# Weight splits put ahead of the tile that each step takes, in a 2-layer hybrid decoder step

## What is computed

```python
h = rmsnorm(x, w['norm1_g'])
(q_m, k_m, v_m, i_pre, f_pre, o_pre, glu_a, glu_b, q_a, k_a, v_a, g_pre) = split_cols(h @ w['w_in'])
y_a = (sigmoid(o_pre) * mlstm(q_m, k_m, v_m, i_pre, f_pre)) @ w['w_mlstm_out']
y_b = silu(layernorm(dwconv(glu_a * sigmoid(glu_b)))) @ w['w_conv_out']
y_c = sliding_window_attention(rope(q_a), rope(k_a), v_a) @ w['w_attn_out']
x = x + (g_a * y_a + g_b * y_b + g_c * y_c) @ w['w_out']
h2 = rmsnorm(x, w['norm2_g'])
gp, up = h2 @ w['w_ffn_gate'], h2 @ w['w_ffn_up']
x = x + (silu(dwconv3(gp)) * up) @ w['w_ffn_down']
```

## Time and profile before

| | us |
|---|---|
| median of 3 runs | 1123.89 (1120.84 to 1132.49) |
| the profiled execution | 1123.45 |
| its span | 1121.7 |
| mean granted TensorE clock in it | 0.968 |
| TensorE busy, 7950 matmuls | 1058.4 (94%) |
| VectorE busy | 795.8 (71%) |
| ScalarE busy | 538.8 (48%) |

### The profile page before, as it was taken

How to read it: one execution, slowest core, us unless ns; L and a number is a source line. 1 busy time by engine, 2 the same in 40 slices (tenths; PEclk the granted TensorE clock), 3 DMA queues, 4 the chain that set the end, 5 groups by cost and what they waited for, 6 DMA issues and landing times.

```text
span 1121.7 us, 19458 instructions
## 1 busy us (share of the span) xinstructions
PE 1058.4 (94%) x7950; PEld 1004.1 (90%) x7950; DVE 795.8 (71%) x1433; ACT 538.8 (48%) x951; POOL 68.0 (6%) x65
## 2 busy tenths in 40 slices
PE   5999999999898999999979999999997989999997
PEld 3988889888798999999979897898887989999996
DVE  4576986855698677775555879777648867887663
ACT  3545553424634555553344555542274536666432
POOL 0020000213100000000000200002230000000000
PEclk9999999989899999999989999999989989999998
DMA  9654545254455575555566564363454547665561
GB/s 259 142 131 119 131 114 151 76 163 101 141 151 150 151 228 170 172 164 170 156 171 150 145 141 128 99 165 94 132 142 129 160 116 235 192 183 168 177 182 46
DMA packets 318498, 168.13 MB, mean 150 GB/s; under 512 B 25174, under 2 KB 317334, under 8 KB 318218
## 3 DMA queue, kind: packets, MB, share of 16 engines
q1 hardware_dynamic: 318266, 165.83, 53.7%
q10 hardware_dynamic: 144, 1.07, 0.2%
HBM read 160.38 MB, written 9.71 MB: 152 GB/s over the span
## 4 chain that ended last, share of the span: by engine, by line
PE 75%; DVE 15%; ACT 4%; issue 4%; DMA 1%; SPq 0%; DVEq 0%
PE ps_tile L845 15%; PE ps_tile L846 14%; PE ps_tile L847 14%; PE work L845 7%; PE work L847 6%; PE work L846 6%; DVE w_lo L1653 5%; ACT w_hi L1223 2%; DVE uc L1753 1%; PE work L1035 1%; DVE prod L1704 1%; ACT scores L1348 1%; PE work L1068 1%; PE work L1048 1%; PE work L1070 1%
## 5 line engine op out<-in xcount | busy, mean ns | idle before, releaser
L1653 DVE TENSOR_TENSOR w_lo<-w_raw,w_hi 128x1024 fp32r<-128x1024 f32 (+1 forms) x288 | 346.7, 1209 | 134.9 <-ACT w_hi L1223 134.2
L1223 ACT ACTIVATE w_hi<-w_raw 128x1024 fp32r<-128x1024 f32 (+1 forms) x288 | 295.1, 1027 | 119.1 <-DMA w_raw<-in_w_ffn_down 67.9
L845 PE MATMUL ps_tile<-h_hi,w_hi 128*128 128x280 f32 (+2 forms) x944 | 285.9, 303 | 10.3 <-DVE h_lo L1663 10.2
L846 PE MATMUL ps_tile<-h_lo,w_hi 128*128 128x280 f32 (+2 forms) x944 | 278.5, 295 | 0.0
L847 PE MATMUL ps_tile<-h_hi,w_lo 128*128 128x280 f32 (+2 forms) x944 | 277.9, 294 | 0.0
L845 PEld LDWEIGHTS ps_tile<-h_hi,w_hi 128*128 128x128 f32 (+1 forms) x944 | 181.3, 192 | 16.8 <-issue 13.8
L846 PEld LDWEIGHTS ps_tile<-h_lo,w_hi 128*128 128x128 f32 (+1 forms) x944 | 181.0, 192 | 1.2
L847 PEld LDWEIGHTS ps_tile<-h_hi,w_lo 128*128 128x128 f32 (+1 forms) x944 | 180.4, 191 | 0.6
L1753 DVE SCALAR_TENSOR_TENSOR uc<-u_pad,vec,uc 128x272 f32<-128x272 f32 x240 | 124.3, 571 | 0.1
L845 PE MATMUL ps_tile<-xg_hi,w_hi 128*128 128x280 f32 (+1 forms) x368 | 107.6, 292 | 7.3 <-DVE x L1710 7.3
L847 PE MATMUL ps_tile<-xg_hi,w_lo 128*128 128x280 f32 (+1 forms) x368 | 107.0, 291 | 0.0
(11 more groups left out here) (338 smaller groups left out, 1934.3 us busy)
## 6 DMA issues: line engine op xcount, KB each, us to landing
w_raw<-in_w_in SPq DMA_DIRECT2D x98, 512.0 KB, 4.0
w_raw<-in_w_ffn_gate SPq DMA_DIRECT2D x44, 512.0 KB, 3.9
w_raw<-in_w_ffn_up SPq DMA_DIRECT2D x44, 512.0 KB, 3.9
w_raw<-in_w_ffn_down SPq DMA_DIRECT2D x32, 512.0 KB, 3.6
w_raw<-in_w_out SPq DMA_DIRECT2D x16, 512.0 KB, 3.6
w_raw<-in_w_ffn_down SPq DMA_DIRECT2D x14, 384.0 KB, 3.4
w_raw<-in_w_in SPq DMA_DIRECT2D x20, 256.0 KB, 3.6
c_head<-in_state_mlstm_c SPq DMA_DIRECT2D x8, 512.0 KB, 3.8
```

The lines of the kernel that those rows point to most:

```text
L845: mm(out, hi[:, k, :], a_hi[:, k0 + k, f:T], start=first, stop=False, skip_group_check=True)
L846: mm(out, hi[:, k, :], a_lo[:, k0 + k, f:T], start=False, stop=False, skip_group_check=True)
L1223: go(h, r, ACT.Copy).then_inc(w_hi_ready, 1)
L1653: tt(lo, r, h.bitcast(F32), ALU.subtract).then_inc(w_split[n % SLOTS], 1)
```

## The change

Both loops now put the splits in front of `take`. `split_at(n)` gives the pieces that step `n` splits: none for a step right behind the first of a group, two (`n + 4` and `n + 5`) for the first of a group, and `n + 4` for all others. In the first step of a group ScalarE's splits stand ahead of `root_mean`, and VectorE's ahead of `inverse_root`. Nothing else is changed: the same instructions with the same operands, in another order on ScalarE and VectorE.

```diff
+def split_at(n):
+
+    if n - 1 in GROUPS:
+        return []
+    ahead = [n + AHEAD, n + AHEAD + 1] if n in GROUPS else [n + AHEAD]
+    return [i for i in ahead if i < N_PIECES]
@@ ScalarE
+                    if n in GROUPS:
+                        for i in split_at(n):
+                            split_hi(i)
                     if n == STEP["gate", 0]:
                         f = first_token(l, "out")
                         root_mean(...)
                         load_table(ACT.Silu, 119)
+                    if n not in GROUPS:
+                        for i in split_at(n):
+                            split_hi(i)
                     for tile in PIECES[n][4]:
                         if LAST_RUN[tile] < RUNS_THROUGH[n]:
                             take(tile)
-                    if n + AHEAD < N_PIECES:
-                        split_hi(n + AHEAD)
@@ VectorE
                     if n == STEP["gate", 0]:
                         second_norm_lo(KD - 1)
+                    for i in split_at(n):
+                        split_lo(i)
+                    if n == STEP["gate", 0]:
                         inverse_root(...)
                     for tile in PIECES[n][4]:
...
                     if n == 18:
                         softmax_sample_2()
-                    if n + AHEAD < N_PIECES:
-                        split_lo(n + AHEAD)
```

## The result

| | before | changed |
|---|---|---|
| median of 4 runs each, us | 1124.67 (1120.84 to 1132.49) | 1184.68 (1177.08 to 1190.45) |
| the profiled execution | 1123.45 | 1190.45 |
| its span | 1121.7 | 1188.6 |

What follows compares the result with a forecast made beforehand. TensorE was taken to bound the kernel, most fully in the FFN, until a closed ScalarE-VectorE round replaced it there. 79.5 us lost less 10 gained is 69.5, added to 1123.45: 1193 us, range 1178 to 1210.

Steps and rivals of the forecast that it cites:

- The ring: FFN pair: ScalarE and VectorE wait for each other in a closed round of 8.06 us, against 6.18 on TensorE.
- What it costs: Both FFNs: the closed round loses 38.2 us in layer 0 and 41.3 in layer 1, 79.5 in all.
- TensorE's wait in a pair: FFN: TensorE waits for `w_lo` by about 1.9 us a pair, from the fourth pair on.
- The clock: FFN: TensorE's idle time absorbs any time at 1.2 GHz below a share of 0.47, so nothing is added.
- Gains: Outside the FFN: earlier splits shorten TensorE's waits at stage borders by 10 us, bounds 0 and 21.8.
- `att_lo`: TensorE's 8.0 us of waits for `att_lo`: 3.5 us gained by ScalarE splitting while it idled for TensorE.
- `h_lo` of the merged sum: In front of the out group, behind ya: TensorE's wait of 2.5 us, really for a split, is gained.
- Rope: Ahead of rope: VectorE splitting earlier gains a further 2 us.
- The gate group: Wait before the gate group: gate 1's split comes 1.0 us sooner a layer, despite about 3.1 us an out step.
- The clock that falls for most of the FFN: Rival: the FFN runs at 1.2 GHz for a share of 0.6, giving 1227 us; chance 0.07.
- One hand-over covered: Rival: one `split_hi` of 1.08 us is not exposed in the FFN round, giving 6.98 and 1150 us; chance 0.07.
- Faster: Rival: ScalarE's splits run ahead, the FFN stays TensorE's and only the gains are left, 1113 us; chance 0.04.

Runs made afterwards that it cites:

- e3: Changed kernel, but in FFN gate steps ScalarE makes the up step's split too, ahead of its silu; 1122.48 us, 0.996 of the kernel before.
- e10: Changed kernel, but in FFN up steps VectorE's split stands behind its up multiply; 1121.01 us, 0.991 of the kernel before.
- e5: Changed kernel plus one unneeded 128x512 ScalarE copy ahead of its split in FFN up steps, from the second pair on; 1210.73 us, one run.
- a2: The changed kernel measured again, unaltered, on another chip; 1187.83 us, 1.051 of the kernel before.
- e1: Changed kernel, but splits go back behind the take on both engines after the first gate step, in FFN and down; 1104.77 us, 0.980 of before.
- e11: Kernel before, with splits in front of the take only in steps 13 to 38 (rope and attention), grouping as before; 1118.75 us, 0.993 of before.
- e7: Kernel before, with splits in front of the take only in steps 55 to 75 (yc to the first gate step); 1122.87 us, 0.995 of before.
- e6: Kernel before, with splits in front of the take only in steps 0 to 54 (projection, attention, mLSTM); 1107.32 us, 0.981 of before.
- e8: Changed kernel, but VectorE's splits are in front only up to the first out step and at the gate group's head; 1097.68 us, 0.975 of before.
- e4: Changed kernel, but VectorE's splits stand behind its takes throughout, ScalarE's stay in front; 1109.49 us, 0.984 of the kernel before.
- e9: As e8, but VectorE's splits in the ya steps also stand behind its takes; 1095.92 us, 0.970 of the kernel before.

## Why the prediction was right, and where it was off

**The ring: right, term by term.** The starts in the changed kernel give, in the order of the prediction's list, 0.53, 0.34, 1.08, 1.14, 0.47, 0.35, 1.07, 1.14 and 1.93 us: 8.05 for a forecast of 8.06, no term off by more than 0.01. The order alone, with hand-overs read from the earlier trace rows, was enough to know it. e3, e10 and e5 moved it to 6.51, 6.52 and 8.56. This is what the forecast rests on, and no luck.

**What it costs: right, and exact by some luck.** 38.2 and 41.3 us were forecast for the two layers, and 38.2 and 41.3 came. The parts were off by up to 0.7 us and cancelled. From the issue of piece 81 to the second pair's last tap it took 8.25 and 8.05 us, for 8.06 and 8.02. The 20 rings took 160.5 and 158.7 us, for 161.2 and 159.2: the last of them is 0.48 us shorter, as the piece that its first split is for has six blocks (128x768, 0.96 us for `split_lo`). And from the end of the last `act_lo` to the end of the third down piece it took 0.9 us in both, for 0.4, since the matmuls behind that wait (3.59 and 3.68 us, the 7.3 us for `act_lo`) ran at 1.2 GHz (0.44 us each in layer 0, where they take 0.29 at the full clock).

**TensorE's wait in a pair: size off.** Forecast were 1.9 us, measured 1.6 (1.7 in layer 1). The count was right: from the fourth pair on, 19 in each layer. The step said that the rest of the ring, 8.06 - 6.18, is idle time. But a pair with a gap in it keeps TensorE busy for longer than 6.18 us: in the window 460 to 540 it was busy for 63.27 us of 80, which is 6.37 in 8.05. Matmuls start 0.13 us apart but are shown for 0.29 each, so the last one ahead of a gap covers 0.16 us of it. And behind the first one after a gap the next starts only 0.23 us later (468.83, 469.06). This moved no end, because the ring sets it. In layer 1, where TensorE's own pair takes 5.93 us and the ring 7.96, the same sum was 2.0 for 1.7.

**VectorE's waits: right.** 1.45 and 0.50 us in front of its two splits, for 1.4 and 0.5, and 43 of them in each layer, for 44.

**The clock: right that it costs nothing in the pairs, wrong in its reading of when it falls.** It was 1.00 over both windows of layer 0 and fell for one stretch in layer 1, in the repeat a2 for three (a mean of 0.97 from 945 to 1117 us); the idle time of the pairs took this up. The prediction read from its two rows that the length of a wait decides. The runs don't bear that out: behind the wait of 2.76 us below the group came to 1.2 GHz, behind 3.54 us before it did not the earlier trace rows, and in e5 2.1 us were enough. The Trainium skill's "TensorE: Matmul & The Clock Gate", Part 1, says that the idle state of the array is the half clock and that activity has to win back the full one. e5 agrees, where gaps of 2.1 us brought the clock down in every second pair. That each pair would start slow by it, as the prediction has it, did not come in the changed kernel: with gaps of 1.6 us in each pair the clock stayed up in layer 0.

**Gains: mis-sized, low by 2.5 us in the trace and by 9 to 13 in the medians.** Forecast were 10. In the trace they are 12.5, between the medians of changed kernel and before 79.5 - 60.0 = 19.5, between those of e1 and before 22.9. This is the main reason why the median lies 8 us below the forecast of 1193. Of its four terms:

- `att_lo`, 3.5: the wait fell by 4.2.
- `h_lo` of the merged sum in front of the out group, 2.5: it fell by 2.0. In its place stands a wait of 0.5 us for `prod`.
- Rope, 2.0: no wait shows it. The one for `probs_t` fell from 2.6 us to 0.8, but it is 2.7 in e1 and 3.2 in e11, which have the new order there too. `km_t` fell by 2.3, but does so in e7 (steps 55 to 75) and not in e6 (0 to 54), so it lies behind rope. The prediction had it in its bounds and not in its sum.
- The gate group, 2.0: wrong. The wait was 7.3 us and is 7.1.

The first matmul of the gate group in layers 0 and 1 of the changed kernel, as in the earlier trace rows, and a later one of layer 0:

```profile
357.48 0.37 PE L853 MATMUL ps_tile<-xg_hi,w_hi 128*128 128x280 f32 x1 [2.76 <-DVE x L1722]
...
358.98 0.43 PE L855 MATMUL work<-xg_hi,w_lo 128*128 128x280 f32 x1
...
932.46 0.56 PE L853 MATMUL ps_tile<-xg_hi,w_hi 128*128 128x266 f32 x1 [4.35 <-DVE x L1722]
```

In layer 0 the gap shrank by 0.8 us (3.54 to 2.76), in layer 1 it grew by 0.5 (3.81 to 4.35). Where 1.0 us a layer was to be gained, the two together gave 0.2. And in layer 0 what the gap gave was taken back at once: the group ran in part at 1.2 GHz (0.43 us a matmul), so that its first matmul came 5.0 us sooner than before but the end of its first piece only 3.4 (368.79 against 372.23).

The step that was mis-sized is the one that set a ring of 3.1 us a step against an earlier place of the split. The ring itself was right. VectorE's split of gate 1, the one that the group waits for, and the add behind it in layer 0, then the same split in layer 1:

```profile
355.89 1.23 DVE L1665 TENSOR_TENSOR w_lo<-w_raw,w_hi 128x1024 fp32r<-128x1024 f32 x1 [0.15 <-ACT w_hi L1231]
357.04 0.44 DVE L1722 TENSOR_TENSOR x<-x,work 128x280 f32<-128x280 f32 x1
...
930.88 1.23 DVE L1665 TENSOR_TENSOR w_lo<-w_raw,w_hi 128x1024 fp32r<-128x1024 f32 x1 [0.18 <-ACT w_hi L1231]
```

Four rounds lie between the split of piece 73 and this one (77). They take 355.89 - 343.38 = 12.51 us in layer 0 and 930.88 - 918.47 = 12.41 in layer 1, or 3.13 and 3.10 each, where before they took 11.54 and 11.30. So the ring costs 1.0 and 1.1 us. The gaps changed by 0.8 less and 0.5 more, so the earlier start of the split of piece 73 was worth 1.8 us in layer 0 but only 0.6 in layer 1. The rest was lost in the first round: ScalarE waited for the DMA of piece 73, issued at the end of the group, for 0.37 us in layer 0 and 1.24 in layer 1, and the two splits at the head held the first add up by some 0.4 and 0.7 us. The prediction named that DMA and took one value for both layers.

e8, with VectorE's old order from the second step of out on, agrees: its four rounds take 11.52 and 11.30 us, and its gaps before the gate group are 1.82 and 2.67 us, 0.9 and 1.7 less than in the changed kernel. Of that 1.0 and 1.1 are the ring, and in layer 1 ScalarE's wait for the DMA was 0.72 us instead of 1.24. With VectorE in the old order throughout (e4) the two gaps sum to 7.4 us, in e8 to 4.5, in the changed kernel to 7.1. So the new order at the head of the out group gains some 2.9 us (e4 and e8 differ in steps 0 to 66 too), and in the other steps of out it loses 2.6.

Of what the medians show beyond the trace, a part is less time at 1.2 GHz, which the prediction didn't look for ahead of the FFN. Its bounds for the gains, 0 to 21.8, were made from waits alone, and e1's 22.9 lies just above them. The remainder has no account.

**One thing was missed and cost nothing that is seen.** The steps of ya close a ring too: ScalarE's splits there stand 4.37 us apart (322.50, 326.88) instead of 3.55. In layer 0 of the changed kernel TensorE has no wait of over 0.3 us in these steps or in front of the out group.

**The rivals.** The clock that falls for most of the FFN (1227): no, it fell for one stretch. One hand-over covered (1150): that is e3 and e10, made on purpose; the ring was then shorter by 1.5 us and not by 1.08, because the silu or the rounding went under VectorE's split as well. Faster (1113): in no FFN with both engines in the new order.

## What to carry to other kernels

When two in-order engines hand data to and fro, list the starts along the circle in which each waits for the other, and sum the hand-overs: if the sum is above the round of the engine that bounds the stage, the circle is the new bound, although no engine is busy. An instruction that can be done early, such as a weight split, is most useful right behind the instruction that the other engine is waiting for; in front of it, it delays both. So the place is chosen by stage: in front of a take that waits for TensorE (a gain of some 2% up to yc), and for VectorE behind it where the take starts a turn of the other engine (shown for the FFN by the times and for out by the waits; for ya it stayed open).

## What the runs showed that was not expected

- Gaps of 1.6 us, one in each 8.05 us, left the granted clock at 1.00 over 160 us in layer 0. Gaps of 1.7 us, one in each 7.96 us, brought it down now and then in layer 1 (once in the changed kernel, three times in a2). Gaps of 2.1 us, one in each 8.56 us, brought it down to 1.2 GHz for a stretch in every second pair (0.90), and the time did not show it, since the ring was the bound.
- The wait before the gate group is put down to the add of `x` (L1722), whose end it follows by 0.00 to 0.03 us, but that add doesn't end it. Before, the add was that of out 7 (`x<-x,ps_tile` at 362.07); in the changed kernel it is that of out 6 (`x<-x,work` at 357.04), which before had ended at 359.63, 2.9 us ahead of the start. What both kernels have in common is the split of gate 1, which ends 0.36 us ahead of the start (362.16 and 362.52, 357.12 and 357.48). The code agrees: `project` waits there for the three splits and for the banks of out 2, 3 and 4, whose adds had long been done. So the prediction read this wait rightly. In the FFN TensorE starts only 0.05 us behind a split (468.78, 468.83); what the other 0.3 us are here is not known.
- A version that beats both kernels has the same instructions as either: e9, 0.970 of the time before.
